# Block 1's expert weights in whole rows, and the last two up chunks by column halves

## The reference, cut to what matters

```
def expert_choice_ffn(h, w_router, w_gate, w_up, w_down):
    B, N, D = h.shape                       # 1, 1024, 1024
    cap = EC_CAPACITY_FACTOR * N // N_EXPERTS   # 128 tokens per expert
    aff = jax.nn.softmax((h @ w_router).astype(jnp.float32), axis=-1)
    g, idx = lax.top_k(jnp.swapaxes(aff, 1, 2), cap)
    xs = jax.vmap(lambda hb, ib: hb[ib])(h, idx)
    hid = jax.nn.silu(jnp.einsum('becd,edf->becf', xs, w_gate)) * jnp.einsum('becd,edf->becf', xs, w_up)
    ys = jnp.einsum('becf,efd->becd', hid, w_down) * g[..., None].astype(h.dtype)
    return jax.vmap(lambda yb, ib: jnp.zeros((N, D), yb.dtype).at[ib.reshape(-1)].add(yb.reshape(-1, D)))(ys, idx)
```

## Time and profile before

| | us |
|---|---|
| median of three runs | 2303.7 (2301.5 to 2305.8) |
| the profiled execution, device time | 2301.8 |
| its span in the trace | 2299.8 |
| PE busy | 2026.0 (88%) |
| DVE busy | 1724.7 (75%) |
| ACT busy | 1246.7 (54%) |
| ring loads of moe_w_gate, issue to landing, median | 11.7 |
| ring loads of moe_w_up | 11.6 |
| ring loads of moe_w_down | 13.8 |

### The profile page before, as it was taken

How to read it: one execution, slowest core, us unless ns; L and a number is a source line. 1 busy time by engine, 2 the same in 40 slices (tenths; PEclk the granted TensorE clock), 3 DMA queues, 4 the chain that set the end, 5 groups by cost and what they waited for, 6 DMA issues and landing times.

```text
span 2299.8 us, 30988 instructions
## 1 busy us (share of the span) xinstructions
PE 2026.0 (88%) x9509; PEld 1675.5 (73%) x9509; DVE 1724.7 (75%) x1899; ACT 1246.7 (54%) x1464; POOL 293.9 (13%) x295
## 2 busy tenths in 40 slices
PE   3999999846999999999598988965999999999990
PEld 2888878735888878778476766854888888888770
DVE  5676664398999999999526544446999999999877
ACT  2311112105888787787514423214888888888762
POOL 1000001100100110110301450101011001010013
PEclk8999999957999999999898999987999999999995
DMA  9276853516999999999631103354999999999986
GB/s 317 71 252 221 274 199 136 217 40 239 381 384 382 382 386 382 379 389 382 243 96 52 37 19 114 120 196 156 404 412 411 412 412 411 412 411 412 374 304 260
DMA packets 240943, 637.07 MB, mean 277 GB/s; under 512 B 19796, under 2 KB 56936, under 8 KB 240876
## 3 DMA queue, kind: packets, MB, share of 16 engines
q1 hardware_dynamic: 209536, 524.35, 60.6%
q0 software_dynamic: 27104, 97.58, 12.0%
q10 hardware_dynamic: 4236, 14.27, 1.6%
HBM read 575.78 MB, written 60.34 MB: 277 GB/s over the span
## 4 chain that ended last, share of the span: by engine, by line
PE 63%; DVE 13%; DMA 10%; SPq 5%; issue 4%; ACT 3%; POOL 1%; ACTq 0%; DVEq 0%; POOLq 0%; PEldq 0%
PE ps L1974 19%; PE ps L1977 18%; PE ps L1975 18%; DMA ring<-in_moe_w_down 7%; SPq L525 5%; DVE mL L1463 1%; PE ps L2385 1%; DMA h_dram<-h2t 1%; DMA ring<-in_ada_w 1%; PE ps L2097 1%; DVE top_i L1446 1%; DVE top_v L1445 1%; DVE affT L1448 1%; DVE xz L1609 1%; PE ps L2232 1%
## 5 line engine op out<-in xcount | busy, mean ns | idle before, releaser
L1847 DVE TENSOR_TENSOR mL<-ring,mH 128x1024 fp32r<-128x1024 f32 x384 | 454.4, 1220 | 38.0 <-ACT mH L1160 34.0
L1463 DVE TENSOR_TENSOR mL<-ring,mH 128x1024 fp32r<-128x1024 f32 x384 | 455.1, 1219 | 33.3 <-ACT mH L988 24.4
L988 ACT ACTIVATE mH<-ring 128x1024 fp32r<-128x1024 f32 x384 | 401.8, 1062 | 100.7 <-PE ps L1977 63.7
L1974 PE MATMUL ps<-mH,xsH 128*128 128x512 f32 x1088 | 437.2, 402 | 7.4 <-DVE mL L1847 4.4
L1977 PE MATMUL ps<-mH,xsL 128*128 128x512 f32 x1088 | 426.7, 392 | 0.0
L1975 PE MATMUL ps<-mL,xsH 128*128 128x512 f32 x1088 | 426.4, 392 | 0.0
L1160 ACT ACTIVATE mH<-ring 128x1024 fp32r<-128x1024 f32 x384 | 390.8, 1054 | 31.5 <-PE ps L1977 31.5
L1974 PEld LDWEIGHTS ps<-mH,xsH 128*128 128x128 f32 x1088 | 205.8, 189 | 48.7 <-issue 7.3
L1977 PEld LDWEIGHTS ps<-mH,xsL 128*128 128x128 f32 x1088 | 205.4, 189 | 45.0
L1975 PEld LDWEIGHTS ps<-mL,xsH 128*128 128x128 f32 x1088 | 205.9, 189 | 39.6
L1974 PE MATMUL ps<-mH,hidH 128*128 128x512 f32 x544 | 217.3, 399 | 13.6 <-DVE hidL L1508 6.6
(11 more groups left out here) (404 smaller groups left out, 3031.7 us busy)
## 6 DMA issues: line engine op xcount, KB each, us to landing
ring<-in_w_expert_gate SPq DMA_DIRECT2D x144, 512.0 KB, 10.8
ring<-in_w_expert_up SPq DMA_DIRECT2D x144, 512.0 KB, 11.3
ring<-in_w_expert_down SPq DMA_DIRECT2D x144, 512.0 KB, 10.5
ring<-in_moe_w_gate SPq DMA_DIRECT2D x128, 512.0 KB, 11.7
ring<-in_moe_w_up SPq DMA_DIRECT2D x128, 512.0 KB, 11.6
ring<-in_moe_w_down SPq DMA_DIRECT2D x128, 512.0 KB, 13.8
ring<-in_ada_w SPq DMA_DIRECT2D x96, 512.0 KB, 5.7
yslot_dram<-xz POOLq DMA_DIRECT2D x31, 512.0 KB, 7.0
```

What stands on the lines that cost most here:

```text
L988: act.activation(mH[:, m % WSETS, :], ring[:, m % RING, :], ACT.Copy).then_inc(S["m1_hi"], 1)
L1463: dve.tensor_tensor(mL[:, m % WSETS, :], ring[:, m % RING, :], mH[:, m % WSETS, :].bitcast(F32), ALU.subtract).then_inc(S["m1_lo"], 1)
L1847: dve.tensor_tensor(mL[:, wset, :], ring[:, slot, :], mH[:, wset, :].bitcast(F32), ALU.subtract).then_inc(S["m2_lo"], 1)
L1974: pe.matmul(o, high, rh, start=start, stop=False)
```

## The change

Gate and up chunks become whole rows, as the down chunks are: chunk c is one k-block of 1024 columns, 4 KB per partition, chunks 0 to 7 gate and 8 to 15 up. So both gate halves are complete after chunk 7, and both up halves only at the end of chunk 15. ACT does one silu over both banks at step 13. PE takes the last two up chunks (LATE = 2) by column halves: column half 0 of chunks 14 and 15 (six matmuls, then `m1_up_half`), then column half 1 of chunk 14 (three), `h_transposes(e, 0)`, column half 1 of chunk 15 (three), `x_transposes`, `h_transposes(e, 1)`, and then the down chunks. DVE's products stand at steps 19 and 20, the splits of the transposed halves at steps 20 and 22 of ACT and DVE. The number of matmuls, transposes, splits and bytes is the same; there is one silu less per expert, over twice the width.

```
@@ SP
-                if c < 16:
-                    n, kp = c // 8, (c % 8) // 2
-                    src = (moe_g, moe_u)[c % 2][e, :, 2 * kp:2 * kp + 2, 512 * n:512 * n + 512]
-                    dst = ring[:, s, :].rearrange("p (k n) -> p k n", k=2)
-                else:
-                    src, dst = moe_d[e, :, c - 16, :], ring[:, s, :]
-                sp.dma_start(dst, src).then_inc(ring_in[s], 16)
+                sp.dma_start(ring[:, s, :], (moe_g, moe_u, moe_d)[c // 8][e, :, c % 8, :]).then_inc(ring_in[s], 16)
@@ ACT
-                if m == 13 or m == 21:
-                    n = m // 21
-                    act.wait_ge(S["m1_used"], 24 * e + 8 * n + 8)
-                    act.activation(sg[:, 512 * n:512 * n + 512], ps[:, n, :], ACT.Silu).then_inc(S["m1_silu"], 1)
-                if m == 19 or m == 23:
-                    j = m // 23
+                if m == 13:
+                    act.wait_ge(S["m1_used"], 24 * e + 8)
+                    act.activation(sg.rearrange("p (a b) -> p a b", a=2), ps[:, 0:2, :],
+                                   ACT.Silu).then_inc(S["m1_silu"], 1)
+                if m == 20 or m == 22:
+                    j = m // 22
                     act.wait_ge(S["m1_hT"], 2 * e + j + 1)
@@ DVE
-                if m == 13 or m == 21:
-                    n = m // 21
-                    dve.wait_ge(S["m1_silu"], 2 * e + n + 1)
+                if m == 19 or m == 20:
+                    n = m - 19
+                    if n == 0:
+                        dve.wait_ge(S["m1_silu"], e + 1)
+                        dve.wait_ge(S["m1_up_half"], e + 1)
+                    else:
+                        dve.wait_ge(S["m1_used"], 24 * e + 16)
                     dve.tensor_tensor(hid[:, 512 * n:512 * n + 512], sg[:, 512 * n:512 * n + 512], ps[:, 2 + n, :],
                                       ALU.mult).then_inc(S["m1_hid"], 1)
-                if m == 19 or m == 23:
-                    j = m // 23
+                if m == 20 or m == 22:
+                    j = m // 22
                     dve.wait_ge(S["m1_hT_hi"], 2 * e + j + 1)
@@ PE
+            def rows_part(m, halves):
+                k, w = m % 8, [slice(512 * n, 512 * n + 512) for n in halves]
+                return three([ps[:, 2 * (m // 8) + n, :] for n in halves], xsH[:, r, k, :], xsL[:, r, k, :],
+                             [(mH[:, m % WSETS, at], mL[:, m % WSETS, at]) for at in w], k == 0, k == KD - 1)
+
             for m in range(24):
-                pe.wait_ge(S["m1_lo"], 24 * e + m + 1)
                 if m < 16:
-                    n, kp, u = m // 8, (m % 8) // 2, m % 2
-                    bank = ps[:, n + 2 * u, :]
-                    if m % 8 == 0 and not first:
-                        pe.wait_ge(S["m1_hid"], 2 * e + n - 1)
+                    if m == 0 and not first:
+                        pe.wait_ge(S["m1_hid"], 2 * e)
                         pe.wait_ge(S["m1_hT_lo"], 2 * e)
-                    for k2 in range(2):
-                        k = 2 * kp + k2
-                        w = slice(512 * k2, 512 * k2 + 512)
-                        last = three([bank], xsH[:, r, k, :], xsL[:, r, k, :],
-                                     [(mH[:, m % WSETS, w], mL[:, m % WSETS, w])], k == 0, k == KD - 1)
+                    if m < 16 - LATE:
+                        pe.wait_ge(S["m1_lo"], 24 * e + m + 1)
+                        last = rows_part(m, (0, 1))
+                    else:
+                        if m == 16 - LATE:
+                            for m0 in range(m, 16):
+                                pe.wait_ge(S["m1_lo"], 24 * e + m0 + 1)
+                                last = rows_part(m0, (0,))
+                            last.then_inc(S["m1_up_half"], 1)
+                        last = rows_part(m, (1,))
                 else:
+                    pe.wait_ge(S["m1_lo"], 24 * e + m + 1)
@@
-                if m == 13:
+                if m == 14:
                     h_transposes(e, 0)
                 if m == 15:
                     if not (static(q) and e == E1 - 1):
                         x_transposes(e + 1, 1 - r, 16 * q + (16 if r == 0 else 32))
-                if m == 17:
                     h_transposes(e, 1)
```

More of the change, by code:

```diff
@@ L21 @@
 ADA_RING = 4
+LATE = 2
 WSETS = 6
@@ L32 @@
     masks var_ready rstd_ready stored m1_tok m1_y_done zero_row rows_zero rows_in small_in
-    silu_ready sq_done mod_ready tr_ready tr_hi split_hi f_part cv_done c_copied route1 e1_exp m1_used m1_hi
+    silu_ready sq_done mod_ready tr_ready tr_hi split_hi f_part cv_done c_copied route1 e1_exp m1_used m1_up_half m1_hi
     m1_xT m1_xT_hi slots_ready m1_silu m1_hT m1_hT_hi if_zero gate_in if_hi v_even gate_exp branch d2_out uc_ready
@@ L262, in build @@
         [("m1_xT_lo", 2 * E1), ("m2_xT_lo", 2 * (E2 + 1 + NOVF))],
-        [("m1_silu", 2 * E1), ("m2_silu", E2), ("ov_silu", NOVF)],
+        [("m1_silu", E1), ("m2_silu", E2), ("ov_silu", NOVF)],
         [("m1_hid", 2 * E1), ("m2_hid", E2), ("ov_hid", 2 * NOVF)],
```

## The result

The changed kernel takes 2306.8 us (median of 20 runs, 2305.0 to 2308.5) beside 2301.9 for the kernel before (20 runs on the same chip). The ratio on record is 1.0016 with an interval of 1.0010 to 1.0023, which is 3.7 us more (2.3 to 5.3); the two medians lie 4.9 us apart, a ratio of 1.0021, within that interval. The forecast was +3.5. The profiled execution has a span of 2304.9 and a device time of 2306.9.

What follows compares the result with a forecast made beforehand. PE bounds the first experts (34.52 us), loads the later ones (35.54); with stalls PE sets 35.22. Fourteen periods +1.3, first expert +0.7, last +1.5: +3.5 us on 2303.7, so 2307.2, own range 2304 to 2310.

Steps and rivals of the forecast that it cites:

- What bounds the kernel: Block 1's experts before the change: first experts PE-bound at 34.52 us, from expert 6 loads set the pace at 35.54.
- Whole rows: Gate and up loads: 416 instead of 391 GB/s, load period from 35.54 to about 34.2 us, at most 8.5 us gained.
- the two rules weighed in the prediction: DMA transfer size: 512 B suffices for line rate, or going from 2 to 4 KB can help; prediction sided with the second.
- The three stalls: PE waits at the end of up chunks for product 0, product 1 and hidL 0: 0.35, 0.23, 0.24, sum 0.82 a period.
- The margin of DVE: DVE before product 0: chunk 18's low part ends at 1.2, product 0 starts at 1.56, 0.3 us to spare.
- rival 2: DVE late for product 0, which waits behind chunk 18's split: period 35.22 + 0.3, time 2312; chance 0.25.
- The fourteen periods: Between token transposes of block 1's experts: 35.22 instead of 35.13 us each, together +1.3 us.
- +0.7 and +1.5: First and last expert, outside the fourteen periods: added stalls of +0.7 and +1.5 us, the last lacking token transposes as cover.
- Rival 1: Load rate unchanged, load period stays 35.54, but the reserve lasts and time is the forecast's, 2307; chance 0.05.
- the reserve: Lead of loads from ring and routing in block 1: 5.8 us, of which 4.5 would be used over fourteen periods.
- Rival 3: Stalls at the end of up chunks mostly hidden, about 0.3 a period: -4.8 us, 2299; chance 0.17.

Runs made afterwards that it cites:

- rows alone: The kernel before with only gate and up loaded as whole rows, old order of work kept (weights meet wrong rows and columns): ratio 0.9969 (0.9960 to 0.9978).
- the moves: Changed kernel with half 0's transposes behind all up matmuls, half 1's behind chunk 17: ratio 1.0030; with low-part wait moved to last two matmuls, 0.9975.

## Why the prediction was right

**What bounds the kernel.** Two regimes, PE-bound at 34.52 and load-bound at 35.54. The kernel with only the load changed showed this directly: 34.52 to the end, no kink.

**Whole rows.** The loads' period was put at 34.2. No run shows it as such; what is shown is that it lies below 34.52 (rows alone) and that 396 GB/s were delivered without a wait. The forecast needed only that it lie below 35.22. Of the two rules weighed in the prediction, the one by which the longer rows would bring nothing isn't what this case shows.

**The three stalls.** 0.35, 0.23 and 0.24 were forecast, 0.33, 0.14 and 0.33 measured: 0.82 and 0.80. The second was too long because transposes start 0.05 after DVE's end (811.01 to 811.06) where I took the 0.15 of a matmul; the third too short by 0.09, because with PE going on earlier hidL 0 still came at its own time, 0.15 ahead of the matmul (811.60 to 811.75). The two errors are one, shifted. The first stall holds the same error, hidden by another: DVE's product 0 started 0.27 after the start of the matmul behind its half (807.90 to 808.17) where 0.20 was taken, and PE's transposes 0.05 after its end instead of 0.15. With these stalls the sum is 34.52 - 0.12 + 0.80 = 35.20; the four transposes behind the first stall take 0.41 (808.91 to 809.32) instead of 0.36, and the period came out at 35.23, where 35.22 was worked out. That it fits to 0.01 is partly luck, since steps that were off by 0.05 to 0.10 each cancel.

**The margin of DVE.** 0.3 us were said to be spare before product 0; DVE idled 0.47 (0.41 in the second, third and last expert). In the first expert there was no margin, and product 0 stood right behind a split, which is rival 2 for once:

```profile
557.02 4.62 DVE L1458 TENSOR_TENSOR mL<-ring,mH 128x1024 fp32r<-128x1024 f32 x4
561.56 0.68 DVE L1501 TENSOR_TENSOR xz<-xz,ps 128x512 f32<-128x512 f32 x1
```

```profile
562.30 0.66 PE L2135 MATMUL ps<-ident,xz 128*128 128x128 f32 x4 [0.47 <-DVE xz L1501]
```

The last matmul ahead of these transposes starts at 561.44, so the stall is 0.63 (from 561.67) instead of 0.33.

**The ends of the stage.** Here a term was left out. The fourteen periods gave +1.46 (493.24 - 491.78; forecast +1.3). The +0.7 and +1.5 for the first and the last expert count the stalls of the new kernel, but set against them a kernel before that has no stall outside the fourteen periods. It has one, ahead of expert 14's fifth down chunk, behind the last mark at 1055.51:

```profile
1063.23 0.47 PE L1974 MATMUL ps<-mH,hidH 128*128 128x512 f32 x1 [0.71 <-DVE hidL L1508]
```

By the periods it is worth 1.02 (35.54 - 34.52), and without it 3.5 becomes 2.5. From the first expert matmul of block 1 to block 2's first transposes the traces give 588.02 (538.57 to 1126.59) and before 585.51 (538.77 to 1124.28), which is +2.5. Behind the last mark it is 69.86 and before 68.77: +1.1. Up to the first mark it is 24.92 and before 24.96, in spite of the stall of 0.63:

```profile
538.57:563.49 24.92, 24.45 (x101) 19.78 (x102) 22.45 (x20) 20.31 (x22) 1.69 (x1) 0.92 0.97 366
```

```profile
538.77:563.73 24.96, 24.96 (x100) 20.36 (x101) 23.20 (x21) 20.96 (x22) 1.69 (x1) 0.89 0.96 365
```

The granted clock over this stretch was 0.92, before 0.89, both between the levels of 1.2 and 2.4 GHz, as PE comes out of the idle routing. PE's first matmuls start 0.43 us apart, later ones 0.23. They stay 0.43 apart up to the start at 542.55, before up to that at 544.03, so the fourteenth matmul starts 4.96 us after the first, before 5.65. These 0.69 hide the stall. Why the clock rose earlier is open.

**The total.** The stage that the change touches gives +2.5 in the traces, where +3.5 was forecast. The spans of the two traces differ by 5.1, and the other 2.6 lie before that stage (-0.2) and in block 2 (+2.8), in code that is the same (last section), so they are no effect that I could put down to the change. That the runs give 3.7, and a median of 2306.8 beside the 2307.2 forecast, is in part luck: the forecast starts from 2303.7, the median of three runs, and the median of twenty is 2301.9.

**The rivals.** Rival 1 (unchanged rate) fell with the rows alone. It was half wrong in its own terms too: with the old loads the reserve lasts nine periods and not fourteen. Rival 2 (late product) is a true mechanism, which adds the delay of product 0 in full; the changed kernel pays it in the first expert and is 0.4 to 0.5 us away from it in the others. Rival 3 (hidden stalls) needed a chain that isn't paid; each was paid. It pointed to what can be had, though: with product 0 covered by matmuls and hidL 0 behind the high-part matmuls, one chain is left, and the period is 34.61.

## What to carry to other kernels

Read a stage's period per iteration from the first to the last: a kink in the middle shows two limits, and an average hides what relieving one of them will give. When an order is changed to feed a faster load, write down for each product the chain (last matmul, elementwise engine, next matmul) and what the matmul engine does meanwhile; what isn't covered is a stall in every iteration. A consumer made of high-part and low-part matmuls needs the low part only for its last matmuls, and a wait put there is covered by the first ones (0.26 us a period here by itself, 0.75 where the moves had been made: 35.36 to 34.61).

## What the runs showed of the hardware that I had not expected

- Transposes that wait for DVE start 0.05 us after its end, matmuls 0.15 after it (811.01 to 811.06, 811.60 to 811.75). The four transposes at 808.91, which waited, take 0.41 until the next matmul starts, and those at 803.49, which didn't, 0.36.
- When the clock rises at the head of the stage hides or adds what one or two stalls cost: the first expert took 24.92 us at a mean granted clock of 0.92 and 24.96 at 0.89, with a stall of 0.63 in the first and none in the second.
- Unchanged code takes different times in different executions. In windows that begin and end at the same instructions of block 2, a stretch ahead of its experts took 256.70 us before and 259.20 after, at clocks of 0.87 and 0.86:

```profile
1332.40:1589.10 256.70, 201.46 (x967) 167.71 (x968) 124.48 (x211) 55.74 (x68) 50.10 (x58) 0.87 0.30 109
```

```profile
1334.60:1593.80 259.20, 200.35 (x966) 167.16 (x967) 124.45 (x211) 55.73 (x68) 50.09 (x57) 0.86 0.30 107
```

  Over the ten traces of this case, the stretch from block 2's first transposes to its first expert matmul takes 459.95 to 465.14 us (before 460.41, after 462.83). And from there to the end it takes 715.1 and 715.5 us in the two traces of the result, but 720.2 to 721.4 in the eight of the experiments, beside which the kernel before is slower too (2307.1 and 2307.4 instead of 2301.9). Why is open in both cases. A difference of spans of 2 to 3 us is therefore no evidence here; the period is.
